# A mixer and product-key expert layer on one core: experts with eight of the 128 second keys left out of 13 heads' row gathers and evaluated densely

## The reference

```python
def peer_ffn(x, w_query, sub_keys, expert_u, expert_v):
    q = (xt @ w_query).reshape(T, PEER_HEADS, 2, PEER_KEY_DIM // 2)
    s = jnp.einsum('thcd,hckd->thck', q, sub_keys).astype(jnp.float32)
    s_top, i_top = lax.top_k(s, PEER_TOPK)
    cand = (s_top[:, :, 0, :, None] + s_top[:, :, 1, None, :]).reshape(T, PEER_HEADS, PEER_TOPK * PEER_TOPK)
    cand_idx = (i_top[:, :, 0, :, None] * PEER_KEYS + i_top[:, :, 1, None, :]).reshape(T, PEER_HEADS, PEER_TOPK * PEER_TOPK)
    g_s, g_pos = lax.top_k(cand, PEER_TOPK)
    e_idx = jnp.take_along_axis(cand_idx, g_pos, axis=-1)
    g = jax.nn.softmax(g_s, -1)
    ...
        u = expert_u[eb]
        h = jax.nn.gelu(jnp.einsum('td,thkd->thk', xb, u).astype(jnp.float32), approximate=False)
        v = expert_v[eb]
        return jnp.einsum('thk,thkd->td', (gb * h).astype(v.dtype), v)
```

## Time and profile before

| | |
|---|---|
| median of 3 runs | 917.62 us (915.48 to 917.87) |
| profiled execution: its own time | 914.1 us |
| profiled execution: its span | 912.2 us |
| TensorE's granted clock, mean | 0.835 of full |
| busy PE, DVE, ACT, POOL | 735.9, 595.9, 412.5, 304.9 us |
| data moved by DMA | 332.21 MB, 364 GB/s on average |

### The profile page before, as it was taken

One profiled execution on the slowest core, in us unless ns is written; L12 is line 12 of the kernel. 1 busy time (PEld: TensorE's weight loads), 2 busy tenths in 40 slices (PEclk: granted clock), 3 DMA queues, 4 the chain that ended last, 5 costly groups with the idle time before them and its releaser, 6 DMA issues.

```text
span 912.2 us, 11716 instructions
## 1 busy us (share of the span) xinstructions
PE 735.9 (81%) x4014; PEld 337.4 (37%) x4016; DVE 595.9 (65%) x1406; ACT 412.5 (45%) x1173; POOL 304.9 (33%) x304
## 2 busy tenths in 40 slices
PE   7999999999959889888797687858667676676774
PEld 6886665656515455333143241414211111111100
DVE  1622861647899988765769476787667666667445
ACT  1144314533578776652445435544343434434333
POOL 0010023002435454534245344444444433344330
PEclk9999999999979899889697879877866657657556
DMA  7633644758999999999999999999999999999993
GB/s 279 256 135 139 222 192 188 314 194 336 421 421 410 418 416 421 420 424 421 416 420 421 422 421 418 422 420 421 421 421 421 421 421 421 421 420 422 420 420 131
DMA packets 46766, 332.21 MB, mean 364 GB/s; under 512 B 6097, under 2 KB 6129, under 8 KB 9969
## 3 DMA queue, kind: packets, MB, share of 16 engines
q0 software_dynamic: 37152, 268.45, 71.0%
q1 hardware_dynamic: 9554, 63.01, 17.8%
HBM read 330.37 MB, written 1.06 MB: 363 GB/s over the span
## 4 chain that ended last, share of the span: by engine, by line
PE 40%; DMA 38%; DVE 9%; ACT 7%; issue 4%; POOL 1%; SPq 0%; POOLq 0%; DVEq 0%; ACTq 0%
DMA late<-in_uv,eidx 21%; DMA ring<-in_uv,eidx 8%; PE ps L1198 8%; DMA wring<-in_uv,eidx 7%; PE ps L794 6%; PE ps L770 6%; PE ps L978 5%; ACT late L1249 3%; DVE late L2033 3%; PE ps L918 3%; PE ps L942 2%; ACT L1249 2%; DMA late<-in_uv,apart 2%; DVE ring L2033 2%; PE ps L777 2%
## 5 line engine op out<-in xcount | busy, mean ns | idle before, releaser
L1249 ACT ACTIVATE late<-late 128x1 f32<-128x1 f32 (+3 forms) x787 | 222.4, 285 | 327.9 <-DVE late L2033 306.2
L1198 PE MATMUL ps<-late 64*64 64x512 f32 x976 | 173.1, 798 | 69.9 <-ACT late L1249 68.8
L1198 PE MATMUL ps<-ring,late 64*64 64x512 f32 x912 | 154.3, 763 | 71.5 <-ACT late L1249 71.3
L2033 DVE CUSTOM_DVE_ANT_0 late<-late,x_sb 128x1024 f32<-128x1024 f32 x122 | 149.4, 1224 | 84.5 <-DMA late<-in_uv,eidx 83.8
L2152 POOL DMA_INDIRECT late<-in_uv,eidx x120 | 134.9, 1124 | 183.3 <-PE ps L1198 172.0
L2033 DVE CUSTOM_DVE_ANT_0 ring<-ring,x_sb 128x1024 f32<-128x1024 f32 x114 | 139.5, 1224 | 77.2 <-DMA ring<-in_uv,eidx 75.9
L2152 POOL DMA_INDIRECT ring<-in_uv,eidx x114 | 123.5, 1083 | 165.1 <-PE ps L1198 146.3
L1198 PEld LDWEIGHTS ps<-late 64*64 64x64 f32 x976 | 32.3, 159 | 179.8 <-ACT late L1249 163.3
L1249 ACT ACT_TABLE_LOAD x69 | 88.5, 1283 | 18.1 <-PE ps L770 10.4
L1198 PEld LDWEIGHTS ps<-ring,late 64*64 64x64 f32 x912 | 29.2, 156 | 171.8 <-ACT late L1249 159.9
L1249 ACT ACTIVATE tmp<-ps 128x512 f32<-128x512 f32 (+4 forms) x77 | 37.6, 495 | 65.2 <-PE ps L770 41.4
(11 more groups left out here) (281 smaller groups left out, 798.8 us busy)
## 6 DMA issues: line engine op xcount, KB each, us to landing
wring<-in_wts SPq DMA_DIRECT2D x13, 2048.0 KB, 7.4
ring<-in_wts SPq DMA_DIRECT2D x2, 2048.0 KB, 10.0
kT<-in_wts SPq DMA_DIRECT2D x4, 1024.0 KB, 9.1
ring<-in_wts SPq DMA_DIRECT2D x3, 1024.0 KB, 10.5
wring<-in_wts SPq DMA_DIRECT2D x2, 1428.0 KB, 5.9
wring<-in_wts SPq DMA_DIRECT2D x2, 1388.0 KB, 6.3
ring<-decay_sums SPq DMA_DIRECT2D x2, 1024.0 KB, 5.5
wkeep<-in_wts SPq DMA_DIRECT2D x1, 2048.0 KB, 13.1
```

Of the source, the lines that this page charges most:

```text
L1198: last = mm(o[t][n * HD:(n + 1) * HD, :], factor[tokens, :], values[tokens, n * 512:(n + 1) * 512], start=start, stop=stop, skip_group_che ...
L1249: return nc.scalar.activation(out, in_, func, **kw)
L2033: V.tensor_tensor_reduce(out=u_row, in0=u_row, in1=h_sb[:, i, :], scale=1.0, scalar=0.0, op0=ALU.mult, op1=ALU.add, accum_out=hdot[:, e, k ...
```

## The change

Experts whose second key is below 8 (`DENSE`) are 1,024 of the 16,384, eight blocks of 128. In 13 of the 16 heads, u = 1 to 13, the gathers leave out rows of such experts: `choose` raises their number by 16,384, and the gather gets a bound above which it skips a row; the gate of such a row is set to zero. A token is exempt where the 16th and the 17th best sum are too close, or where the list of candidates may hide a further one.

All 1,024 experts are then evaluated for all 256 tokens. SP loads u and v of the eight blocks, sixteen transfers of 0.52 MB, into homes that weights leave free. PE multiplies a block's u by the hidden state (`dH`) and ACT takes gelu. Gates are rebuilt from the scores of each of the 13 heads (`DENSE_HEADS`): DVE makes eight thresholds, ACT eight exponentials over the 128 first keys (`powers`), DVE keeps those over the threshold (`chosen`), POOL scales by the head's softmax sum and adds to the tile's gates (`dense_sum`). PE transposes the gates (`dT`), DVE multiplies them by gelu (`dW`), and PE adds times v into the same PSUM sums (`dV`). Only then can a tile be finished, so `finish`, `cross` and `root` of tile 0 move to steps 250 to 254. For the new thresholds `choose` finds the next best sum and a few small values for every head but the first.

```diff
@@
-CHOOSE_STEPS = [2, 2, 2, 2, 2, 1, 2, 1, 1, 1, 2, 1, 1, 1, 1]
+CHOOSE_STEPS = [2, 2, 2, 2, 2, 1, 2, 1, 1, 2, 4, 5, 2, 2, 1]
+DENSE = 8
+DENSE_HEADS = [(126, 1), (132, 8), (138, 2), (145, 9), (151, 3), (157, 10), (163, 4), (169, 5), (175, 11), (181, 6),
+               (187, 12), (193, 7), (203, 13)]
@@ def step_tables():
-    for part, k in enumerate((132, 133, 135, 136)):
+    for n, (k, u) in enumerate(DENSE_HEADS):
+        put("dve", k, "thresholds", n, u)
+        put("act", k + 1, "powers", n, u)
+        for part in range(2):
+            put("dve", k + 2 + part, "chosen", n, u, part)
+        put("pool", k + 14, "gates", n, u)
+    for b in range(DENSE):
+        for part in range(4):
+            put("pe", 130 + 9 * b + part, "dH", b, part)
+        put("act", 135 + 9 * b, "dH", b)
+        put("pe", 210 + 5 * b, "dT", b)
+        put("dve", 211 + 5 * b, "dW", b)
+        for i in range(NT):
+            put("pe", 213 + 5 * b + i, "dV", b, i)
+    for part, k in enumerate((251, 252, 253, 254)):
         put("dve", k, "finish", part)
     for part in range(2):
-        put("act", 131 + part, "cross", part)
-    put("act", 134, "root", 36, 7)
+        put("act", 250 + part, "cross", part)
+    put("act", 253, "root", 36, 7)
@@ SP, behind the last weights
+            for n in range(2 * DENSE):
+                if n == 0:
+                    await_full(sp, "mixA", 1, 1)
+                elif n == 2:
+                    await_full(sp, "q", 1, 1)
+                elif 4 <= n < DENSE + 4:
+                    await_full(sp, "H", n - 4)
+                elif n >= DENSE + 4:
+                    sp.wait_ge(values_added, n - DENSE - 3)
+                sp.dma_start(dense_homes[n % 4], dense[:, n * D:(n + 1) * D]).then_inc(dense_here[n % 4], 16)
@@ PE
+            def dense_transposes(b):
+                pe.wait_ge(gates_added, len(DENSE_HEADS))
...
+            def dense_values(b, i):
+                w = dense_home(DENSE + b)
+                await_taken(pe, "G", b)
+                for t in range(2):
+                    at = i * P + t * HD
+                    for n in range(2):
+                        last = mm(ps[n * HD:(n + 1) * HD, Y_BANK[i] + t, :], dense_w[b % 2][:, at:at + HD], w[:, n * 512:(n + 1) * 512],
+                                  start=False, stop=i == 0 and b == DENSE - 1, skip_group_check=True)
@@ ACT
+            def dense_powers(n, u):
+                act.wait_ge(theta_ready, n + 1)
+                if n:
+                    act.wait_ge(gates_added, n)
+                for b in range(DENSE):
+                    last = f(powers[:, b, :], s_all[:, u * 2 * NKEY:u * 2 * NKEY + NKEY], ACT.Exp, bias=shift[:, n % 2, b:b + 1])
+                last.then_inc(powers_ready, 1)
@@ DVE, choose()
                 elif part == 9:
-                    step(V.max_index(gpos[:, 0, 8:16], gtop[:, 8:16], cand2))
+                    V.max_index(gpos[:, 0, 8:16], gtop[:, 8:16], cand2)
+                    step(V.match_replace(cand, gtop[:, 8:16], cand2, BELOW))
+                    step(V.max(next8, cand))
                 elif part == 10:
...
+                    tt(edge, cand[:, TOPK - 1:TOPK], cand[:, TOPK * (TOPK - 1):TOPK * (TOPK - 1) + 1], ALU.min)
+                    step(tt(largest, top[:, 0, 0:1], top[:, 0, 0:1], ALU.mult))
...
+                    step(tt(limit, gtop[:, TOPK - 1:TOPK], next8[:, 0:1], ALU.subtract))
+                    V.tensor_scalar(largest, largest, 2.0 ** -36, None, ALU.mult)
+                    step(tt(limit, limit, limit, ALU.mult))
+                    step(V.scalar_tensor_tensor(clear, limit, largest, inside, ALU.is_gt, ALU.mult))
+                    step(V.tensor_scalar(away, clear, -2e38, 1e38, ALU.mult, ALU.add))
...
+                    if u in dense_of:
+                        V.scalar_tensor_tensor(number, eij[:, 0, :], float(NKEY), eij[:, 1, :], ALU.mult, ALU.add)
+                        step(V.tensor_scalar(left_out, eij[:, 1, :], DENSE - 0.5, clear, ALU.is_lt, ALU.mult))
+                        step(V.tensor_scalar(fetched, left_out, -1.0, 1.0, ALU.mult, ALU.add))
+                        V.scalar_tensor_tensor(eidx[:, par, :], left_out, float(NEXP), number, ALU.mult, ALU.add).then_inc(idx_ready, 1)
@@ DVE, beside the steps
+            def dense_chosen(n, u, part):
+                if part == 0:
+                    dve.wait_ge(theta_ready, n + 1)
+                    dve.wait_ge(powers_ready, n + 1)
+                first = s_all[:, u * 2 * NKEY:u * 2 * NKEY + NKEY]
+                for b in range(part * DENSE // 2, (part + 1) * DENSE // 2):
+                    last = V.scalar_tensor_tensor(powers[:, b, :], first, theta[:, n % 2, b:b + 1], powers[:, b, :], ALU.is_ge, ALU.mult)
+                last.then_inc(chosen_ready, 1)
@@ POOL
+            def dense_sum(n, u):
+                pool.wait_ge(chosen_ready, 2 * (n + 1))
+                total = dense_gates[u // PH].rearrange("p b e -> p (b e)")
+                chosen = powers.rearrange("p b e -> p (b e)")
+                if n in FIRST_OF:
+                    last = G.tensor_scalar(total, chosen, parts_of[:, u:u + 1], None, ALU.mult)
+                else:
+                    pool.wait_ge(gates_added, n)
+                    link(G.tensor_scalar(chosen, chosen, parts_of[:, u:u + 1], None, ALU.mult))
+                    last = G.tensor_tensor(total, total, chosen, ALU.add)
+                last.then_inc(gates_added, 1)
...
-                    G.indirect_dma_start(row(slots[g]), None, uv, bass.IndirectOffsetOnAxis(eidx[:, u % 2, k:k + 1], 0)).then_inc(row_here[slots[g]], 16)
+                    G.indirect_dma_start(row(slots[g]), None, uv, bass.IndirectOffsetOnAxis(eidx[:, u % 2, k:k + 1], 0),
+                                         bounds_check=NEXP - 1, oob_is_err=False).then_inc(row_here[slots[g]], 16)
```

123 lines of the change are left out of this document (107 added, 16 removed).

## The result

The changed kernel takes **978.00 us** (974.57 to 980.26, four runs) against 917.57 (915.48 to 917.87): a ratio of 1.066, 95% interval 1.0625 to 1.0696. I had forecast 936, at most 954. The direction was right, the size was wrong by 42 us. The profiled execution took 980.26, its span is 978.5.

A forecast was written before the change was run, and what follows sets the result against it. The DMA engines, full in the expert stage, were taken as the bound. Terms -4 + 16 + 3 + 3.6 = +18.6 on the profiled 914.1 gave 932.7, forecast as 936 on the runs' scale; 8 in 10 from 906 to 954.

The forecast's parts named there:

- The bound, and the way the time is lost: Likeliest case, chance 0.50: from step 126 DMA falls below full and DVE waits for ACT and POOL; 924 to 954 us.
- the time from gather to dot product: Sign expected from step 126 on: near 6 us if DMA runs dry, 10 us or more of queue if DMA stays full.
- All transfers: Sixteen dense loads of 0.52 MB at 1.25 us each: +19.9 us.
- After step 208: Steps after 207: four more dense transfers, 5.0 us, against 3 of rows, less hidden PE jobs: +3 us (0 to 5).
- The stretch 126 to 207 together: 81 steps, 13 heads: DVE with its waits exceeds the DMA's 15.4 us a head; +16 us taken.
- The waits in part: Steps 126 to 207: DVE's wait for ACT and exclusion by POOL taken between half and all, as they fall at different steps: +16.
- All waits in full: Steps 126 to 207: 1.9 us for ACT plus 2.7 beside POOL a head; 47 us over, 33 after 14 of backlog.
- POOL's scaling: POOL's scaling of 1,024 columns in each dense head: 1.2 us, from a copy of 512 columns at 0.6.
- The backlog of 14 us: Lag that DVE, ACT, PE and POOL may build before the DMA runs dry, some 14 us after step 160.
- Steps before 126: Early steps: rows saved 20.8 us evenly, two transfers 2.5, DVE 9 us more in steps 16 to 63: -4 in all.
- Rows left out: Gathers of thirteen heads: 1,870 rows skipped, 36.3 us if even, 25.1 at the middle deal, the fullest engine setting the pace.
- The end: Token tile 0's finish moved to steps 251 to 254 delays the last dot product: +3.6 us (2 to 6).

The follow-up runs named there:

- two buffers: Changed kernel with a second buffer for ACT's powers, so ACT waits for POOL's sum of the head before last: 958.71 us.
- Choosing alone: Kernel before the change with only the longer `choose`, no rows left out and no dense work: 923.18 us, 1.0077 of before.
- the clumped pattern: Changed kernel without dense work; in the n-th head, partitions numbered n modulo 15 skip all 16 rows (1,792 rows in all): 905.84 us, 0.9890 of the kernel before.
- the even pattern: Changed kernel without dense work, skipping every fifteenth place of step plus partition, exempt tokens kept (1,683 rows): 887.62 us, 0.9720 of the kernel before.

## Why the forecast was wrong

**The bound, and the way the time is lost: right.** DVE over the DMA's pace in the stretch, DMA below full, DVE waiting for ACT, long dot products beside POOL: all there. One sign of it failed: the time from gather to dot product is not near 6 us but 22.6 at step 160, as the rows wait for DVE and not DVE for them. Without the rebuild the stretch is as long as before (207.4, 207.9), so rows and transfers nearly cancel in it, though each at two thirds of its price: rows give 10.2 there (208.9 to 198.7; forecast 15.4), transfers take 11.0 (196.5 to 207.5; forecast 12.5, for ten where the trace has four before the stretch, eight in it and four behind). All transfers cost 21.0 (19.9 forecast). After step 208 it is +2.3 in the trace (+3), and that is luck: without the rebuild it is +7.1, and 4.8 of backlog come off. The rule of the Trainium skill, "SBUF — State Buffer", SBUF: two separate sides, that GpSimd and a VectorE operation with two SBUF inputs exclude each other, agrees with the trace: the dot product that starts 0.04 us after POOL's addition ends 1.08 after it. DVE's operations are lengthened by 34.4 us in all, and by none when POOL's sum is gone.

**The failed step is "The stretch 126 to 207 together": +16.** The stretch is 56 us longer in the trace, and the rebuild costs 51.2 in the runs. Two things in the term were wrong, each shown by a run, and a third was mis-sized:
- *The waits in part.* All waits in full had come to 33, half of each to 8, and I took 16, hoping that they miss each other. With two buffers, so without the wait that I hadn't listed, the rebuild costs 31.9 (958.71 less 926.85), the 33 of all waits in full: its lengthened operations are 2.7 us a head and DVE's wait 1.5, together 4.3 where "in full" was 4.6.
- *A wait that I hadn't listed.* ACT's powers wait for POOL's sum of the head before, in one buffer, and that sum stands in POOL's queue behind waits for PE. It costs the other 19.3, by the second buffer. The diff shows it in one line (`act.wait_ge(gates_added, n)`); I had counted what queues behind DVE's wait and not what ACT waits for.
- *POOL's scaling.* 2.87 us against 1.2, which I had from a copy of 512 columns: the scaling with a scalar per partition is dearer than that copy, and than the addition. So the 2.7 us a head of lengthening that I named as most came about partly by luck: by my own reckoning (POOL's time less 0.8) it would be 4.4 at POOL's real 5.2, and some six tenths of that came.

The backlog of 14 us was of the right kind, but it is paid back behind step 208: 10.1 in the kernel with the sum on DVE, 4.8 in the changed one. The 33 had it taken off within the stretch, so that the sum comes out near 31.9 is in part luck too.

**"Steps before 126": -4, measured +7.** Choosing alone is 7 us late there (582.7 against 575.5), where DVE has little room in the early steps, and the skipped rows give back 6.7 of the 20.8 that their number promised (576.0). That leaves next to nothing; the dense transfers, four by then and not two, add 3.7 (575.4 to 579.1 without the rebuild), and the last 3 or so are the scatter of this trace.

**"Rows left out": 25.1 forecast, 19.8 measured.** The number was off a little and the rule was off a lot. I had overlooked that a token is exempt when either of two corners of its list is picked (5.4% of them), and had taken tile 1's heads in the wrong order: with both mended the reference's inputs give 1,775 rows, against 1,774 in the trace. And I let the fullest engine of the whole kernel set the pace, which the clumped pattern contradicts. The Trainium skill, "DMA: Bandwidth & Descriptors", The descriptor swizzle, says which engine serves which partitions. By its deal, as an estimate, the engine that saves least saves 86 of the 1,775 rows over the whole kernel, but those that save least in each single head sum up to 15; the even pattern has 96 and 80. The clumped pattern has 80 and 0. At 0.31 us a row the totals would set the three 3 to 5 us apart in all (24.8 clumped, 26.7 by key, 29.8 even); measured are 17.3, 19.8 and 35.6. By sums over heads it is 0, 4.7 and 24.8, in the order and with the wide gap measured, but 11 to 17 us too low. So neither rule gives the sizes. That the engine with most left to do in each short stretch sets the pace is my reading of the order, not shown; over how many gathers it evens out was not measured.

**"The end": 3.6 forecast, 0.8 measured.** In the trace of the changed kernel much of the finish lies in the 1.25 us that DVE has free in each late step:

```profile
953.24 1.23 DVE L2186 CUSTOM_DVE_ANT_0 wring<-wring,x_sb 128x1024 f32<-128x1024 f32 x1 [1.25 <-DMA wring<-in_uv,eidx]
...
955.63 0.68 DVE L2175 COPY tmp<-ps 64x512 f32<-64x512 f32 x1 [1.16 <-PE ps L1294]
...
965.23 1.22 DVE L2186 CUSTOM_DVE_ANT_0 late<-late,x_sb 128x1024 f32<-128x1024 f32 x1
966.38 0.08 DVE L2186 DVE_READ_ACCUMULATOR2_ANT late<- 128x1 f32 x1
969.29 0.68 DVE L2175 COPY tmp<-ps 64x512 f32<-64x512 f32 x1 [2.83 <-PE ps L1249]
```

DVE runs without a pause from 955.6 to 966.4, but behind its last dot product it waits 2.83 us for PE, where it waited 2.54 before. The finish alone cost 0.8 us in the runs (in its trace the last dot product starts 1.3 later), so DVE's work there moves the end by little.

## What to carry to other kernels

For every new buffer ask who must be done reading before it is written again, and in which queue that reader stands; a long operation that stands behind waits for a third engine passes them on. Two waits of one engine that each fit its slack don't miss each other by chance: take both in full, above all where a wait of one delays the other. The price of an operation is read from a row of that operation, not of a near one. What a saving of transfers is worth depends on how it is spread: here as many rows gave 35.6 us spread evenly and 17.3 in clumps, so count it over short stretches and not over the kernel. An engine that is full where the saving falls keeps it.

## What the hardware showed that I had not expected

- A row that a gather skips by its bound leaves a 4-byte packet (37,152 packets, 268.45 and 253.93 MB), and skipping saves the row's full time when the skipped rows are spread: 35.6 us for 1,683 rows, against 32.6 by 0.31 us a row and engine.
- GpSimd scales 1,024 columns by a per-partition scalar in 2.87 us, and adds two tensors of 1,024 in 2.36 (1.89 where both are the same tensor); VectorE does both at once in 1.28.
- Beside GpSimd, VectorE operations on one small tensor and a one-column scalar are stretched too: 128 x 8 `TENSOR_SCALAR` from 0.23 to 1.41 and 1.83 us.
